# Decode step of a hybrid decoder layer: decode query from raw panels ahead of the dense projections

## What is computed

```python
h = rmsnorm(x, g); z = h @ w_in                       # fq, fk, fv, ff, gq, gk, gv, gr, gg
o_fox = fox_prompt(fq, fk, fv, logf)                  # prompt: causal, 8 heads of 128
o_fox = fox_sample(fq, fk, fv, logf, k_past, v_past, logf_past)   # decode: 2048 past keys per batch row
S_new, o_gla = gla_chunk(state, gq, gk, gv, glog)     # gated linear attention, 4 heads
x = x + concat(o_fox, norm(o_gla) * silu(gr)) @ w_out
mk, mv = rmsnorm(mem, g_mem) @ w_xk, ... @ w_xv       # 256 memory tokens of the prompt
```

## Time and profile before

| | us |
|---|---|
| median of 3 runs (lowest, highest) | 1661.57 (1658.47, 1665.24) |
| the profiled execution | 1656.92 |
| its span | 1655.2 |
| PE busy, share of the span | 1519.4, 92% |
| DVE busy | 1034.0, 62% |
| ACT busy | 617.6, 37% |
| POOL busy | 229.0, 14% |
| DMA moved | 388.42 MB, 235 GB/s on average |

### The profile page before, as it was taken

One profiled execution on the slowest core, in us unless ns is written; L12 is line 12 of the kernel. 1 busy time (PEld: TensorE's weight loads), 2 busy tenths in 40 slices (PEclk: granted clock), 3 DMA queues, 4 the chain that ended last, 5 costly groups with the idle time before them and its releaser, 6 DMA issues.

```text
span 1655.2 us, 32624 instructions
## 1 busy us (share of the span) xinstructions
PE 1519.4 (92%) x12197; PEld 1399.3 (85%) x12197; DVE 1034.0 (62%) x3234; ACT 617.6 (37%) x725; POOL 229.0 (14%) x331
## 2 busy tenths in 40 slices
PE   4999987899998898996779999999999999999997
PEld 4999854577776677995579999999999999999996
DVE  4579899898977876656455555553445555554444
ACT  3343233232143553443344333333333333333443
POOL 3011222222222222330120000000000000000221
PEclk9999989899998999998789999999999999999998
DMA  8558999999998899453225555544555555553553
GB/s 318 178 186 304 402 365 404 404 372 375 379 387 295 294 377 402 167 179 120 77 102 178 177 180 184 185 163 146 185 175 204 180 180 184 186 182 123 183 182 122
DMA packets 78979, 388.42 MB, mean 235 GB/s; under 512 B 9096, under 2 KB 9872, under 8 KB 56864
## 3 DMA queue, kind: packets, MB, share of 16 engines
q1 hardware_dynamic: 35424, 230.90, 39.1%
q0 software_dynamic: 39376, 143.15, 23.1%
q10 hardware_dynamic: 4080, 13.12, 2.0%
HBM read 377.03 MB, written 10.10 MB: 234 GB/s over the span
## 4 chain that ended last, share of the span: by engine, by line
PE 75%; DVE 13%; DMA 5%; ACT 4%; issue 3%; POOLq 0%; ACTq 0%; DVEq 0%; SPq 0%; POOL 0%
PE bank L1554 23%; PE bank L1555 22%; PE bank L1556 22%; DVE page L1084 4%; DVE wlo L1028 2%; DMA page<-kc_dram 2%; PE bank L1711 2%; DMA page<-vc_dram 1%; DVE wlo L993 1%; ACT whi L602 1%; DMA raw<-p_out_dram 1%; ACT whi L565 1%; DMA raw<-p_in_dram 1%; DVE rstd L1019 1%; PE bank L1886 1%
## 5 line engine op out<-in xcount | busy, mean ns | idle before, releaser
L1554 PE MATMUL bank<-hh,whi 128*128 128x264 f32 (+1 forms) x2368 | 693.5, 293 | 36.2 <-DVE wlo L1028 23.5
L1555 PE MATMUL bank<-hl,whi 128*128 128x264 f32 (+1 forms) x2368 | 677.4, 286 | 0.0
L1556 PE MATMUL bank<-hh,wlo 128*128 128x264 f32 (+1 forms) x2368 | 677.1, 286 | 0.0
L993 DVE TENSOR_TENSOR wlo<-raw,whi 128x2048 fp32r<-128x2048 f32 (+1 forms) x174 | 356.2, 2047 | 281.4 <-ACT whi L565 281.4
L1554 PEld LDWEIGHTS bank<-hh,whi 128*128 128x128 f32 x2368 | 452.7, 191 | 72.9 <-issue 38.7
L565 ACT ACTIVATE whi<-raw 128x2048 fp32r<-128x2048 f32 (+1 forms) x174 | 299.3, 1720 | 545.0 <-PE bank L1556 537.6
L1555 PEld LDWEIGHTS bank<-hl,whi 128*128 128x128 f32 x2368 | 453.2, 191 | 0.5 <-issue 0.2
L1556 PEld LDWEIGHTS bank<-hh,wlo 128*128 128x128 f32 x2368 | 450.7, 190 | 0.0
L1084 DVE CUSTOM_DVE_ANT_0 page<-page,qb 128x128 f32<-128x128 f32 x1024 | 226.4, 284 | 18.3 <-ACT qb L647 11.3
L1554 PE MATMUL bank<-f_hi,whi 128*128 128x264 f32 x704 | 202.2, 287 | 7.5 <-DVE f_lo L1526 7.5
L1556 PE MATMUL bank<-f_hi,wlo 128*128 128x264 f32 x704 | 201.5, 286 | 0.0
(11 more groups left out here) (295 smaller groups left out, 1441.9 us busy)
## 6 DMA issues: line engine op xcount, KB each, us to landing
raw<-p_gu_dram SPq DMA_DIRECT2D x88, 1024.0 KB, 4.9
page<-kc_dram POOLq DMA_DIRECT2D x128, 512.0 KB, 8.6
page<-vc_dram POOLq DMA_DIRECT2D x128, 512.0 KB, 9.1
raw<-p_in_dram SPq DMA_DIRECT2D x48, 1024.0 KB, 8.3
raw<-p_dn_dram SPq DMA_DIRECT2D x64, 704.0 KB, 4.1
raw<-p_out_dram SPq DMA_DIRECT2D x16, 1024.0 KB, 5.5
raw<-p_mem_dram SPq DMA_DIRECT2D x8, 1024.0 KB, 8.3
x_res<-x_fm_dram SPq DMA_DIRECT2D x8, 528.0 KB, 10.3
```

The costliest lines, as they stand in the source:

```text
L993: tt(wlo[:, (k + 2) % 4, 0:blocks * P], raw[:, (k + 2) % 4, 0:blocks * P], whi[:, k % 2, 0:blocks * P], ALU.subtract).then_inc(S("w_split" ...
L1554: mm(out, blk(whi, k % 2, b), rh, start=start, stop=False)
L1555: mm(out, blk(whi, k % 2, b), rl, start=False, stop=False)
L1556: return mm(out, blk(wlo, k, b), rh, start=False, stop=stop)
```

## The change

The decode query is computed first and alone. DVE scales the 8 decode tokens by the gain (`xg`). For each of the 8 query panels, as soon as its raw data has landed, PE multiplies `xg` (8 columns, stationary) by the 16 raw blocks (moving) in fp32, block b into the column group b % 4. A matmul with the constant `K_SUM` adds the four partial sums, twice over (rows 0 to 7 and 32 to 39); ACT writes the high part, scaled by 1/rms, and DVE the low part. There is no cast, split or transpose for it. The sums of squares, which stood behind the first dense panel, now stand behind the fifth query panel. The narrow weights' high and low parts move from ahead of turn 0 into its first slot.

The dense query panels come later: each fox head's query, value and key panels follow each other. They are loaded a second time, so that SP loads 56 input panels instead of 48, and all 48 dense input panels lie in the turns. `QUARTERS` has 224 quarters now: 32, 32, 20, 20, 28, 28, 20, 28 and 16 per turn. The memory tokens begin in slot 6 of turn 7 (`MEM_AT`), eight chunks a slot, with two slots without a quarter, and their squares have three buffers instead of one. Heads 6 and 7 start in slots 26 and 27 instead of 23 and 24, counted from turn 6.

```diff
+IN, TURNS = 56, 9
+DECODE_Q = 8
+QUARTERS = ([2] * 16,) * 2 + ([1, 1, 1, 2] * 4,) * 2 + ([2, 2, 2, 1] * 4,) * 2 + ([1, 1, 1, 2] * 4, [2] * 6 + [0, 0] + [2] * 8, [1] * 16)
+MEM_AT = 6
+HEAD_AT = (0, 2, 6, 8, 12, 17, 26, 27)
...
+TILE = [None] * DECODE_Q + [*range(24, 28), *range(32, 40), *range(28, 32), *(8 * s + h for h in range(8) for s in (0, 2, 1)), *range(44, 48), *range(40, 44)]
+def weight_row(p):
+    return p - DECODE_Q if p >= DECODE_Q else 16 + 3 * p
...
+    k[:, K_SUM:K_SUM + 40] = (r[:, None] % 32 == np.arange(40)[None, :] % 32) & (r[:, None] % 32 < ND)
...
-            first_x(0)
-            first_x(1)
-            weights(0)
-            first_x(2)
-            first_x(3)
-            for p in range(1, IN):
+            for g in range(4):
+                first_x(g)
+            for p in range(IN):
                 weights(p)
...
-                if g == 0:
-                    panel_cast(0)
-            panel_cast(1)
+            act.sem_inc(S("w_hi"), DECODE_Q)
+            def query_sum(n):
+                act.wait_ge(S("mm_done"), 4 * n + 4)
+                act.activation(t_sb[:, 512 * n:512 * n + 512], bank[2 + n][:, :], ACT.Copy).then_inc(S("rows16"), 1)
+            def query_hi(n):
+                act.wait_ge(S("rows_ps"), n + 1)
+                act.wait_ge(S("sel"), 1)
+                act.activation(q16[:, 512 * n:512 * n + 512], bank[4 + n][0:40, :], ACT.Copy, scale=sm8[0:40, 61:62]).then_inc(S("s16_hi"), 1)
...
+            query_sum(0)
             act.wait_ge(S("head_in"), HEAD)
             norm_root(0, T)
+            query_hi(0)
+            query_sum(1)
+            query_hi(1)
+            panel_cast(DECODE_Q)
...
                     q_copy(0)
+                    panel_cast(DECODE_Q + 1)
+                    act.wait_ge(S("params_in"), PARAMS)
+                    act.activation(n_hi[:, :], n_raw[:, :], ACT.Copy).then_inc(S("nw_hi"), 1)
...
-                if j < 4:
-                    if j % 2 == 0:
-                        act.wait_ge(S(f"w_in{j // 2}"), 16 * (IN // 4 + 1))
-                    for c in range(4 * j, 4 * j + 4):
+                if j in (0, 1):
+                    act.wait_ge(S(f"w_in{j}"), 16 * (IN // 4 + 1))
+                    for c in range(8 * j, 8 * j + 8):
                         norm_hi(1, c, 2, hh, mem_raw(c), MEM)
...
+                if j == 1:
+                    panel_cast(IN + 1)
...
+                    if p == IN - 1:
+                        act.wait_ge(S("mm_done"), p + 1)
+                    else:
+                        panel_step(p)
+                if t == 7 and j >= MEM_AT:
+                    memory_turn(j - MEM_AT)
...
+            for n in range(2):
+                ch.link(dve.memset(bank[2 + n][:, :], 0.0))
+            dve.wait_ge(S("gains_in"), 16)
+            for g in range(4):
+                dve.wait_ge(S(f"group_in{g}"), 16)
+            ch.link(tt(xg, x_res[:, :, DEC], colv(gains[:, 0, :]).broadcast_to([P, C, ND]), ALU.mult))
+            dve.sem_inc(S("w_split"), DECODE_Q)
...
+            select(0, 32)
+            panel_split(DECODE_Q)
+            query_lo(0)
+            query_lo(1)
...
+                if t < ND:
+                    k_page(t, j)
                 if g == 0:
-                    token_lo(1, z[:, 4:8, DEC], 4, 2)
-                    select(0, 1)
-                elif t < ND:
-                    k_page(t, j)
+                    panel_split(DECODE_Q + 1)
+                    dve.wait_ge(S("nw_hi"), 1)
+                    tt(n_lo[:, :], n_raw[:, :], n_hi[:, :], ALU.subtract).then_inc(S("nw_lo"), 1)
...
+            def decode_query(p):
+                pe.wait_ge(S("w_split"), DECODE_Q)
+                pe.wait_ge(S(f"w_in{p % 4}"), 16 * (p // 4 + 1))
+                for b in range(C):
+                    g = b % 4
+                    last = mm(bank[2 + p // 4][32 * g:32 * g + ND, P * (p % 4):P * (p % 4) + P], xg[:, b, :],
+                              blk(raw, p % 4, b), start=b < 4, stop=b >= C - 4)
+                last.then_inc(S("mm_done"), 1)
+            def query_rows(n):
+                pe.wait_ge(S("rows16"), n + 1)
+                mm(bank[4 + n][0:40, :], kst[:, K_SUM:K_SUM + 40], t_sb[:, 512 * n:512 * n + 512], start=True, stop=True
+                   ).then_inc(S("rows_ps"), 1)
...
-            for p in range(8):
-                for q in range(4):
-                    quarter(p, q)
-                if p == 0:
+            for p in range(DECODE_Q):
+                decode_query(p)
+                if p == 4:
                     pe.wait_ge(S("head_in"), HEAD)
...
                 if p == 5:
-                    q_rows(0)
+                    query_rows(0)
+            query_rows(1)
+            pe.wait_ge(S("n_lo_done"), C)
...
-                if 2 <= j < 6:
-                    g = j - 2
+                for g in ((0, 1), (2, 3))[j - 1] if j in (1, 2) else ():
                     pe.wait_ge(S("n_sq"), g + 1)
```

More of the change, by code:

```diff
@@ L613, in _, with token_hi, token_rows @@
                     norm_hi(0, c, 0, hh, x_res[:, c, :], T)
-                if g == 0:
-                    panel_cast(0)
-            panel_cast(1)
+            act.sem_inc(S("w_hi"), DECODE_Q)
[6 more added lines that the diff above has]
+                act.activation(q16[:, 512 * n:512 * n + 512], bank[4 + n][0:40, :], ACT.Copy, scale=sm8[0:40, 61:62]).then_inc(S("s16_hi"), 1)
+            def token_hi(n, src, step):
+                act.activation(s16[1][:, 4 * n:4 * n + 4 * step, 0:8], src, ACT.Copy).then_inc(S("s16_hi"), 1)
+            def token_rows(n):
+                act.wait_ge(S("rows_ps"), 3 + n)
+                act.activation(v16[:, 512 * n:512 * n + 512], bank[6 + n][0:16, :], ACT.Copy).then_inc(S("rows16"), 1)
+            query_sum(0)
             act.wait_ge(S("head_in"), HEAD)
             norm_root(0, T)
-            act.wait_ge(S("params_in"), PARAMS)
-            def token_hi(n, src, step):
-                act.activation(s16[1][:, 4 * n:4 * n + 4 * step, 0:8], src, ACT.Copy).then_inc(S("s16_hi"), 1)
[L625 to L639, removed]
+            query_hi(0)
+            query_sum(1)
+            query_hi(1)
+            panel_cast(DECODE_Q)
             def q_copy(t):
@@ L1059, in token_lo, with select, query_lo @@
                 tt(s16[1][:, rows, 8:16], src, s16[1][:, rows, 0:8], ALU.subtract).then_inc(S("s16_lo"), 1)
-            def select(b, value):
-                tt(sel[:, :], ident[0:16, b:b + 1].broadcast_to([16, P]), ident[0:16, b + 8:b + 9].broadcast_to([16, P]), ALU.add
+            def select(b, lo):
+                n = lo + ND
+                tt(sel[0:n, :], ident[0:n, b:b + 1].broadcast_to([n, P]), ident[0:n, lo + b:lo + b + 1].broadcast_to([n, P]), ALU.add
                    ).then_inc(S("sel"), 1)
[L1066 to L1071, removed]
-                    token_lo(0, z[:, 0:4, DEC], 4, 1)
+            def query_lo(n):
+                dve.wait_ge(S("s16_hi"), n + 1)
+                lo = q16[32:40, 512 * n:512 * n + 512]
+                stt(lo, bank[4 + n][32:40, :], sm8[32:40, 61:62], lo, ALU.mult, ALU.subtract).then_inc(S("s16_lo"), 1)
+            dve.wait_ge(S("head_in"), HEAD)
+            norm_scale(0, T)
+            ch.link(tt(sm8[0:40, 48:56], kst[0:40, K_SUM:K_SUM + ND], rstd[0:40, DEC], ALU.mult))
+            ch.link(dve.tensor_reduce(sm8[0:40, 60:61], sm8[0:40, 48:56], AX.X, ALU.add))
+            ch.link(ts(sm8[0:40, 61:62], sm8[0:40, 60:61], SCALE, None, ALU.mult))
+            select(0, 32)
+            panel_split(DECODE_Q)
+            query_lo(0)
+            query_lo(1)
             tail4 = tail[:, :].rearrange("p (h b j) -> p j b h", h=H, b=ND)
@@ L1273, in memory_turn @@
             def memory_turn(j):
-                if j < 4:
-                    for c in range(4 * j, 4 * j + 4):
+                if j < 2:
+                    for c in range(8 * j, 8 * j + 8):
                         norm_lo(1, c, 2, mem_raw(c), hh, hl, MEM)
-                elif j == 7:
+                elif j == 4:
                     norm_scale(1, MEM)
@@ L1608, in norm_sum @@
                 mm(bank[6][:, 0:T], ones, s_sq[:, (C - 1) % 2, :], start=False, stop=True).then_inc(S("n_ss"), 4)
-            def q_rows(n):
-                pe.wait_ge(S("s16_lo"), n + 1)
-                for h in range(4):
-                    last = pe.transpose(bank[2 + n][0:16, P * h:P * h + P], s16[0][:, 4 * n + h, :], ident)
-                last.then_inc(S("rows_ps"), 1)
+            def decode_query(p):
[10 more added lines that the diff above has]
+                   ).then_inc(S("rows_ps"), 1)
             def v_rows():
@@ L1728, in state_turn @@
                     for n in range(2):
-                        last = mm(bank[2 + n][:, :], sel[:, :], v16[:, 512 * n:512 * n + 512], start=True, stop=True)
+                        last = mm(bank[2 + n][:, :], sel[0:16, :], v16[:, 512 * n:512 * n + 512], start=True, stop=True)
                     last.then_inc(S("gd_v"), 1)
```

(10 more changed lines are left out.)

77 lines of the change are left out of this document (30 added, 47 removed).

## The result

The changed kernel takes 1677.84 us (median of 4 runs, 1675.35 to 1682.8) against 1660.77 us for the kernel before on the same chips: the ratio on record is 1.0122, 95% interval 1.01 to 1.0144 (the two medians alone divide to 1.0103). It is slower, by 17 us between the medians. The forecast was 1658 us and its range ended at 1672.

What follows compares the result with a forecast made beforehand. PE was taken to bound turns 0 and 1, DVE and DMA turns 2 and 3, with mixed limits later. An earlier start saves 27 us, turns 0 to 7 give back 24: 1658 us, no measurable change, range 1638 to 1672.

Steps and rivals of the forecast that it cites:

- The start: Before turn 0: transfers and PE's chain both end near 45 us, 9.6 us follow, turn 0 begins at 55, saving 27 us.
- the hand-overs: In the chain before turn 0: eight passes between engines of about 0.15 us each, by estimate.
- rival 3: Before turn 0: PE's clock stays low from panel 4 on, +7 us, 1665 us in all; chance 0.09.
- Turns 0, 1, 4 and 5: Turns with +4, −4, +4 and +4 quarters, forecast at 70.7, 59.8, 66.8 and 66.0 us.
- the bound by bytes: Turn 1: PE would give 57.7 us, but its transfers at 386 GB/s were to take 59.8, which was taken.
- turn 7's: Turn 7, +12 quarters: PE busy 75.5 us plus 5.5 of waits for the memory norm and panel, 81.0 us.
- the sum to the end of turn 8: The start plus turns 0 to 8: 654.6 us against 657.9 before, −3.3 us, with everything after untouched.
- Turns 2, 3 and 6: Turns 2 and 3, +8 quarters each, forecast at 66.2 us each by DVE; turn 6, −4 quarters, at 63.0.
- DVE's 66.2 us: Turns 2 and 3: 60.8 us plus 5.4 of DVE work for two more panels, above 65.5 by DMA.
- Rival 2: Turn 7's memory join: ACT queued behind late memory panels holds PE, 8 and 6 us, 1672 us in all; chance 0.13.
- the cover I gave it: First memory panel in turn 7: two slots of 4.4 us, hiding a 6 us landing; trouble from about 9 us.
- Rival 1: Later turns: PE's idle holes take the moved work whole, turns 2 and 3 at 62.4 us each, 1643 in all; chance 0.30.

## Why the prediction was wrong, point by point

**The start was right in its sum, partly by luck.** Turn 0 was forecast at 55 us and began at 54.7; panel 4 came at 28.5 us and a query panel took 1.9 us there, as said. Behind it errors cancel. The norm sums took 8.2 instead of 7.1 us, and panels 5 to 7 took 1.0 instead of 1.9 us each. The root, the reciprocal and the selection, which I had cost at nothing beside those panels, held the second row sum instead: 5.3 us on ACT and DVE. The first quarter took 2.97 instead of 1.45 us and the spread 1.15 instead of 0.7, while the hand-overs, whose 0.15 us I had from no row, took 0.03 to 0.11. So rival 3's slow clock was there at about 3 us of its 7 (1.1 + 1.5 + 0.45), hidden by terms that I had set too high.

**Turns 0, 1, 4 and 5 were right** within 2 us each (70.4, 58.0, 67.3, 64.4 against 70.7, 59.8, 66.8, 66.0). In turn 1 the bound by bytes that I took did not hold: PE was busy for 57.25 of 58.0 us.

**The step that failed is turn 7's.** I wrote that "DVE's split then waits for a cast behind the next 8 chunks", and priced that wait only through the second half of the norm, 5.5 us in all. I did not list what else stands behind the split on DVE: the softmax copy on which PE's extraction hangs. PE stood idle for 18.1 us there (4.7 + 13.4) instead of 5.5. Turns 7 and 8 make 16 of the 23 us by which the sum to the end of turn 8 (654.6 against 677.8) was off, and these gaps 12.6 of the 16. A smaller part is the clock: it was granted at 0.60 from 551 to 568.5 us, while PE was idle for most of the time, and of the norm sums behind that gap the first 16 records took 5.83 us and the next 16 took 3.65. The run with that one split moved won 10 us.

**Turns 2, 3 and 6** missed by 3.0, 4.7 and 3.1 us. The main cause is the same order: turn 6 is 62 us with splits last, and turns 2 and 3 take 65.7 to 68.5 us in the three versions with splits last and whole panels, against 66.2 forecast and 69 to 71 measured. A smaller one is a size. I counted 25.3 MB for both turns, which is turn 2's old rate; by turn 3's own 400 GB/s it is 26.4 MB, and 68.4 us at 386 GB/s. The changed kernel moved 26.1 and 26.8 MB in them (377 and 378 GB/s). So in turn 3 the bytes, not DVE's 66.2 us, were the larger term, and the run with 7.9 MB less (ten panels of 1.05 MB, three quarters of each) moved the two turns by 7 us.

**Rival 2 named the place and the sign, not the mechanism.** It asked for a landing above 9 us. The first memory panel landed 7.7 us after its issue, inside the cover I gave it. ACT still waited 8.4 us for it and PE 4.7, since the small sum was queued on DVE behind the split; rival 2 had looked for such steps on ACT alone. The larger gap came from the cast of the second panel. It was given 0.13.

**What held.** Once the splits stand last, the changed kernel takes 1655.2 us, near the 1658 of the sum. That is another kernel, and the nearness is in part chance: its profiled execution, the slowest of ten, needs 659.8 us to the end of turn 8 instead of 654.6. What the sum had right is the trade: the early query moves PE's work, pays for it in new query matmuls and doubled loads, and ends within 0.5% of the kernel before. By medians it is 0.1 to 0.3% slower than the old kernel in the same order. Rival 1 is answered too: the holes of turns 2 and 3 did not take the work whole.

## What to carry to other kernels

In a program whose engines each run a fixed list, a long instruction that waits for another engine lends its wait to everything listed behind it; put the waiting, bulky step last in its slot and the small steps that another engine hangs on first. When a schedule is changed, write down for each wait that grows what stands behind it in its queue and who waits for that; here it was a 0.17 us copy, PE stood idle for 13.4 us, and moving one split won 10. Work moved out of a start-up phase is paid again where it lands (here nearly in full), unless the engine that is idle there is idle for lack of that work and not of bytes.

## What the runs showed of the hardware

A DVE product of 128 x 128 values took 6.17 us in the changed kernel, beside four POOL products of 128 x 1056 values, and ended 0.2 us after the last of them. Alone it took 0.29 us. The three lines are the product beside POOL's work, that work, and the product alone:

```profile
11.32 6.17 DVE L1067 TENSOR_TENSOR xg<-x_res,gains 128x128 f32<-128x128 f32 x1 [8.92 <-DMA x_res<-x_fm_dram]
```

```profile
9.68 7.65 POOL L459 TENSOR_TENSOR x_sqs<-x_res 128x1056 f32<-128x1056 f32 x4
```

```profile
13.06 0.29 DVE L1069 TENSOR_TENSOR xg<-x_res,gains 128x128 f32<-128x128 f32 x1 [10.66 <-DMA x_res<-x_fm_dram]
```

The Trainium skill (SBUF — State Buffer, "Terms") says that VectorE and GpSimd share one pair of ports, held for a whole instruction, and that the loser is blocked instead of sharing; these lines agree, though here the block outlasted single POOL instructions of about 1.9 us. In the kernel before, the first split beside the same POOL work took 7.66 us, where later splits take 2.29: it began at 13.41 us, the POOL products ended at 18.91, and it ended 2.2 us after them.

PE also waited for landing V pages from turn 2 to the end of turn 7: 12.4 us in the kernel before, 6.3 in the changed kernel, 11.3 with splits last. Only the run with 7.9 MB less to load in turns 2 and 3 took that away (1.0 us).
